# A mixture-of-experts step on one core: the order of the weight loads of each turn, the slot of the last fixed expert, and the place of the sort that orders the experts

## The chip, the cores and the metric

The kernel runs as one program on one core of a Trainium2 chip. The metric is the device time in microseconds of one execution, the median of three runs of the kernel before. Everything is 32-bit floating point.

## The reference

One step of a two-layer backbone over 128 context tokens and 128 latent tokens, 1024 wide. Each layer mixes tokens (retention, differential attention, latent attention), then runs a mixture of experts. Only the second half matters here:

```python
scores = jax.nn.sigmoid(x @ router_w)              # (256 tokens, 64 experts)
sel = scores + router_bias                          # best 4 of 8 groups, then top 6 experts
gates = scores[eidx] / sum * ROUTED_SCALE
for e in experts:                                   # 64 experts, hidden width 256
    y += gate_e * (silu(x_e @ w_gate[e]) * (x_e @ w_up[e])) @ w_down[e]
y += swiglu(x, sh_w_gate, sh_w_up, sh_w_down)       # shared expert
x = x + gate2 * y
```

Each expert has three matrices of 1 MiB (gate, up, down). All 64 experts of both layers are read: 384 MiB. Which tokens go to which expert is known only at run time.

## The kernel before

Below, a *block* is one of those 1 MiB matrices, moved by one DMA. All blocks are issued by SyncE (SP), whose DMA queue serves them.

**Rounds.** A layer's experts are done in 22 rounds. Experts 0 to 3 are fixed and fill rounds 0 and 1, two experts each. Then come ten turns of two rounds: a *quad round* (four experts, at most 32 tokens each) and a *pair round* (two experts, at most 64 tokens each). The 60 experts of the turns are sorted by token count at run time, and the sorted list `order_i` names the expert that a load takes.

**Slots.** There are five places for an expert's three blocks. A quad round uses slots 0, 1, 2, 3. A pair round uses slot 4 (the fifth: `fifth_gate`, `fifth_up`, `fifth_dn`) and slot 0. So slot 0 is loaded twice in a turn: for the quad, and for the pair's second expert. Slots 1, 2, 3 and 4 are loaded once. That is 18 blocks a turn. In what follows Q0 to Q3 are the quad's experts, P4 and P0 the pair's, and a part is named behind them, as in "P0 up".

**TensorE in a round** (`expert_round`, L1808 to L1861; the matmuls of gate and up are L1832, those of down L1861). Gate matmuls, up matmuls, the first half of the next round's token gather (L1764), the scatter of the round before (L1771), transposes (L1399), the second half of the gather, and then the down matmuls. Two rounds of a layer have something *between* the scatter and the transposes: the pair round of turn 1 runs the shared expert's up matmuls (L1729), and the pair round of turn 2 its down matmuls (L1808). TensorE tells SyncE three things in each round: gate done, up done, down done (`used[0]`, `used[1]`, `used[2]`).

**SyncE in a turn** (the loop at L629). A slot's part may be loaded once the round that used it has said that it is done with it. SyncE is in order: what stands behind a wait is not issued before it. The expert's number comes into a register by `expert_in` (L469), a read of `order_i` in on-chip memory. The loop's body first reads seven of them.

**The start of a layer's experts.** The first three fixed experts are loaded before the router runs. The last one waits for the normalised activations: its gate goes into `fifth_gate`, its down into `fifth_dn`, its up into the first half of a `gu` slot, which the shared expert's gate weights occupy until `sh_gate` (L596 to L600). Meanwhile VectorE ranks the experts (L1284 to L1286, semaphore `ranked`), TensorE multiplies the ranking out (L1756, `ordered`) and VectorE writes `order_i` (L1293, `order_ready`).

Of the kernel before, what the change touches and what calls it, by code (L numbers as in the profile page):

```python
# [31 lines left out]
NC_ = D // P  # L32
G = 2
# [13 lines left out]
E = 64  # L47
GROUPS = 8
TOP_G, TOP_K = 4, 6
FF = 256  # L50
# [4 lines left out]
FIXED = 4  # L55
TURNS = 10
QUAD_CAP, PAIR_CAP = 32, 64
ROUNDS = 2 + 2 * TURNS
PER_TURN = 6
# [7 lines left out]
def quad_at(m):  # L67
    return FIXED + PER_TURN * m


def pair_at(m):
    return FIXED + PER_TURN * m + 4
# [4 lines left out]
CO = {n: P * i for i, n in enumerate(CONSTS)}  # L77
COL = {"i+1": 0, "C-i": 1, "C-1-i": 2, "i": 3, "eps": 4, "sel": 5, "first": 13, "cap": 16}
# [86 lines left out]
def trunk(nc, t, out):  # L165
    ctx = ExitStack()
    with ctx:
# [7 lines left out]
        RING = 4  # L175
        gu = sb("gu", [P, RING, 2 * NC_ * FF])
        dn = sb("dn", [P, RING, 2, D])
        cst = sb("cst", [P, FIRST_W])
# [110 lines left out]
        key_row, above, chosen = (hit[0:E, E * n:E * n + E] for n in range(3))  # L289
# [13 lines left out]
        fifth_gate = xh[:, 0].rearrange("p c t -> p (c t)")  # L303
        fifth_up, fourth_up = carve(NC_ * FF), carve(NC_ * FF)
        fifth_dn = carve(2 * D).rearrange("p (j n) -> p j n", j=2)
        fourth_dn = carve(2 * D).rearrange("p (j n) -> p j n", j=2)

        PS = ctx.enter_context(nc.psum_tensor("PS", [P, 8, 512], F32))
# [56 lines left out]
        S = {n: sem(n) for n in names}  # L365
# [12 lines left out]
        item_slot, expert_slot = {}, []  # L378
# [88 lines left out]
        def expert_in(sp, l, at):  # L467

            return sp.value_load(order_i[0:1, l, at], min_val=0, max_val=E - 1)  # L469
# [28 lines left out]
        def _(sp):  # L498
            def gate_or_up(l, x, half):
                return t[f"exp_w_{('gate', 'up')[half]}"][l, bass.ds(x, 1)].rearrange("e (p c) n -> (e p) (c n)", c=NC_)  # L500
# [20 lines left out]
            def load_fixed_dn(j, l):  # L521
                sp.dma_start(dn_block(j if j < RING - 1 else RING), down(l, j)).then_inc(S["fixed_dn_in"], 16)

            def load_quad(j, l, x, part):
                if part == 2:
                    sp.dma_start(dn_block(j), down(l, x)).then_inc(S["quad_dn_in"], 16)
                else:
                    sp.dma_start(gu_block(j, l, part), gate_or_up(l, x, part)
                                 ).then_inc(S["quad_up_in" if part else "quad_gate_in"], 16)

            def load_pair(j, l, x, part):
                if part == 2:
                    sp.dma_start(dn_block(j), down(l, x)).then_inc(S["pair_dn_in"], 16)
                else:
                    sp.dma_start(gu_block(j, l, part), gate_or_up(l, x, part)
                                 ).then_inc(S["pair_up_in" if part else "pair_gate_in"], 16)
# [3 lines left out]
            for l in range(DEPTH):  # L540

                for n in range(starts[l], ends[l]):
# [8 lines left out]
                    slot = item_slot[n]  # L551
# [39 lines left out]
                    if j == 2:  # L591
                        load_fixed_dn(2, l)

                last, slot = FIXED - 1, expert_slot[l][RING - 1]
                sp.wait_ge(S["h_a"], NC_ * (2 * l + 2))
                sp.wait_ge(S["h_d"], NC_ * (2 * l + 2))  # L596
                sp.dma_start(fifth_gate, gate_or_up(l, last, 0)).then_inc(S["last_fixed_in"], 16)
                load_fixed_dn(last, l)
                sp.wait_ge(S["sh_gate"], l + 1)
                sp.dma_start(gu[:, slot, 0:NC_ * FF], gate_or_up(l, last, 1)).then_inc(S["last_fixed_in"], 16)  # L600


                r0, used = ROUNDS * l, [S[n] for n in ("gate_done", "up_done", "down_done")]
                sp.wait_ge(S["order_ready"], l + 1)
                xs = [expert_in(sp, l, slice(quad_at(0) + j, quad_at(0) + j + 1)) for j in range(4)]
                xf = expert_in(sp, l, slice(pair_at(0), pair_at(0) + 1))
                xp = expert_in(sp, l, slice(pair_at(0) + 1, pair_at(0) + 2))

                load_quad(3, l, xs[3], 1)
                load_pair(RING, l, xf, 1)  # L610
                load_quad(3, l, xs[3], 2)

                for part in range(3):
                    sp.wait_ge(used[part], r0 + 1)
# [4 lines left out]
                load_pair(RING, l, xf, 0)  # L619
                sp.wait_ge(used[1], r0 + 2)  # L620
                load_quad(2, l, xs[2], 1)
                load_quad(3, l, xs[3], 0)
                sp.wait_ge(used[2], r0 + 2)
                load_quad(2, l, xs[2], 2)
                load_pair(RING, l, xf, 2)
                for part in range(2):
                    sp.wait_ge(used[part], r0 + 3)
                    load_pair(0, l, xp, part)
                with sp.Fori(0, TURNS - 1) as m:  # L629
                    xs = [expert_in(sp, l, bass.ds(m * PER_TURN + (quad_at(1) + j), 1)) for j in range(4)]  # L630
                    xl = expert_in(sp, l, bass.ds(m * PER_TURN + (pair_at(0) + 1), 1))
                    xf = expert_in(sp, l, bass.ds(m * PER_TURN + pair_at(1), 1))
                    xp = expert_in(sp, l, bass.ds(m * PER_TURN + (pair_at(1) + 1), 1))

                    for part in range(2):
                        sp.wait_ge(used[part], m * 2 + (r0 + 3))
                        for j in range(1, 4):
                            load_quad(j, l, xs[j], part)
                    sp.wait_ge(used[2], m * 2 + (r0 + 3))
                    load_pair(0, l, xl, 2)  # L640

                    for part in range(2):
                        sp.wait_ge(used[part], m * 2 + (r0 + 4))
                        load_quad(0, l, xs[0], part)
                    for j in range(1, 4):
                        load_quad(j, l, xs[j], 2)
                    sp.wait_ge(used[2], m * 2 + (r0 + 4))
                    load_quad(0, l, xs[0], 2)
                    for part in range(2):
                        load_pair(RING, l, xf, part)  # L650

                        sp.wait_ge(used[part], m * 2 + (r0 + 5))
                        load_pair(0, l, xp, part)
                    load_pair(RING, l, xf, 2)
                xl = expert_in(sp, l, slice(pair_at(TURNS - 1) + 1, pair_at(TURNS - 1) + 2))
                sp.wait_ge(used[2], r0 + ROUNDS - 1)
                load_pair(0, l, xl, 2)
                over_loads(sp, l)


# [273 lines left out]
        def _(v):  # L934
# [81 lines left out]
            for l in range(DEPTH):  # L1016
# [208 lines left out]
                for g in range(G):  # L1225
                    for a in range(GROUPS):
                        last = v.max(gtop[:, g, a], selv[:, g, 8 * a:8 * a + 8])
# [33 lines left out]
                r0, g0, s0_ = ROUNDS * l, ROUNDS * l, ROUNDS * l  # L1261
# [10 lines left out]
                def one_hot(b, n, at, fixed=False):  # L1272

                    return tt(onehot[b].rearrange("p g (e s) -> p g e s", e=n), iota_of(n),
                              fixed_columns(posu, n, at) if fixed else columns(pos, n, at), ALU.is_equal)
# [4 lines left out]
                              fixed_columns(score, n, at) if fixed else columns(wgt, n, at), ALU.mult)  # L1280

                v.tensor_copy(counts, PS[0:E, 6, 0:2])
                one_hot(0, 2, 0, True).then_inc(S["sel_ready"], 1)
                link(ts(above, key_row, key_col, None, ALU.is_gt))  # L1284
                link(v.tensor_reduce(rank, above, AX.X, ALU.add))
                ts(chosen, cst[0:E, order + E:order + 2 * E], rank, None, ALU.is_equal).then_inc(S["ranked"], 1)  # L1286
                settle("ranked")
                v.wait_ge(S["sel_ready"], s0_ + 1)
                gate_it(0, 2, 0, True).then_inc(S["gated_ready"], 1)
                one_hot(1, 2, 2, True).then_inc(S["sel_ready"], 1)  # L1290
# [104 lines left out]
        def _(pe):  # L1395
# [66 lines left out]
            for l in range(DEPTH):  # L1462
# [264 lines left out]
                def shared_part(bank, u, j, ks):  # L1727
                    for k in ks:
                        ins = mmul(PS[:, bank, j * T:j * T + T], w[:, u, k, j], hT[:, k, :], start=(k == 0),  # L1729
                                   stop=(k == NC_ - 1))  # L1730
                    return ins
# [11 lines left out]
                ins.then_inc(S["tallied"], 1)  # L1743

                shared_part(5, 0, 1, range(4))
                pe.wait_ge(S["weighed"], l + 1)
                pe.wait_ge(S["placed"], l + 1)
                for a, x in enumerate((posu, score)):
                    for g in range(G):
                        ins = turn(PS[0:E, 7, (2 * a + g) * P:(2 * a + g + 1) * P], x[:, g])  # L1750
                ins.then_inc(S["counted"], 1)
                shared_part(5, 0, 1, range(4, NC_)).then_inc(S["sh_gate"], 1)

                pe.wait_ge(S["ranked"], l + 1)
                pe.wait_ge(S["h_tok_a"], G * (l + 1))
                mmul(PS[0:2, 2, 0:E], cst[0:E, CO["cols"] + COL["i"]:CO["cols"] + COL["i"] + 2], chosen,  # L1756
                     start=True, stop=True).then_inc(S["ordered"], 1)

                r0, g0 = ROUNDS * l, ROUNDS * l

# [51 lines left out]
                def block_of(x):  # L1812
                    return x.rearrange("p (k n) -> p k n", k=NC_)
# [6 lines left out]
                def expert_round(m, u, gus, dns, gates_in, ups_in, downs_in, last=False, between=None):  # L1820
# [37 lines left out]
                    for n in range(2):  # L1858
                        for j in range(2):
                            for h, weights in enumerate(dns):  # L1860
# [5 lines left out]
                own = [gate_up(j) for j in range(RING)]  # L1866
                fixed_in = [(gu_loaded[expert_slot[l][j]], fixed_at[l][j]) for j in range(RING - 1)]
                expert_round(0, 0, own[0:2], (dn[:, 0], dn[:, 1]), fixed_in[0:2], [], (S["fixed_dn_in"], 64 * l + 64))
                expert_round(0, 1, (own[2], (block_of(fifth_gate), own[3][0])), (dn[:, 2], fifth_dn),
                             [fixed_in[2], (S["last_fixed_in"], 32 * l + 32)], [], (S["fixed_dn_in"], 64 * l + 64))  # L1870
                t0 = TURNS * l + 1
                quad_gus = own[0:3] + [(own[3][0], block_of(fourth_up))]
# [120 lines left out]
```

## Time and profile before

| what | value |
|---|---|
| median of three runs | 1432.39 us (1431.57 to 1439.19) |
| the profiled execution, its own time | 1434.13 us |
| its span in the trace | 1432.3 us |
| TensorE matmul busy | 1289.1 us (90%) |
| VectorE, ScalarE busy | 287.6 us, 239.4 us |
| bytes moved | 496.18 MB, mean 346 GB/s |
| mean granted TensorE clock | 0.939 of full |
| chain that ended last | PE 69%, DMA 23% |

A busy TensorE is not one at its peak, and an engine that waits for data still shows a high share when the clock is low while it works. A DMA is shown twice: when its queue issues it, and, in the view of the DMA issues, how long it took from there until its data had landed. The profiled execution is 1.7 us above the median.

### The profile page before, as it was taken

The page shows a single profiled execution, that of the slowest core. Times are in us where ns is not written, and L with a number is a line of the kernel's source. Part 1 is how long each engine was busy: PE and PEld are TensorE (multiplying, and loading weights), DVE is VectorE, ACT ScalarE, POOL GpSimd, SP SyncE. Part 2 cuts the span into 40 slices and gives each one's busy share as a digit, 9 for nine tenths or more (in the row PEclk, how much of TensorE's full clock was granted, in tenths as well). Part 3 has the DMA queues.
Part 4 walks back from the last instruction along what each step waited for, and adds up shares of the span by engine and source line. Part 5 has one row for each costly group of instructions (what it writes and reads, how often), then busy time and mean ns, then how long its engine had stood idle before and what let it go on. Part 6 is the DMA issues. An engine that isn't in the chain of part 4 may idle for free.

```text
span 1432.3 us, 23390 instructions
## 1 busy us (share of the span) xinstructions
PE 1289.1 (90%) x9852; PEld 886.9 (62%) x9852; DVE 287.6 (20%) x694; ACT 239.4 (17%) x500; POOL 2.6 (0%) x13
## 2 busy tenths in 40 slices
PE   5999989999997998889999988999999888889886
PEld 2665678766674655556566557876676645556554
DVE  1306414111101101011041442321101101011012
ACT  1112513111000110010130253211100000001001
POOL 0000000000000000000000000000000000000000
PEclk8999779999998999999899997999999989999998
DMA  9866636989999999999973671398999999999992
GB/s 392 318 248 257 258 147 265 381 355 420 421 420 422 422 422 422 422 422 422 392 262 136 244 312 60 164 387 337 422 421 421 421 422 421 422 421 422 423 421 94
DMA packets 81026, 496.18 MB, mean 346 GB/s; under 512 B 10560, under 2 KB 12864, under 8 KB 24640
## 3 DMA queue, kind: packets, MB, share of 16 engines
q1 hardware_dynamic: 76752, 492.68, 84.2%
q10 hardware_dynamic: 4208, 2.52, 0.6%
q8 instruction: 53, 0.87, 0.2%
q14 instruction: 13, 0.11, 0.0%
HBM read 493.17 MB, written 2.00 MB: 346 GB/s over the span
## 4 chain that ended last, share of the span: by engine, by line
PE 69%; DMA 23%; DVE 3%; ACT 3%; issue 1%; SPq 0%; DVEq 0%; ACTq 0%
DMA dn<-in_exp_w_down 20%; PE PS L1832 15%; PE PS L1861 12%; PE PS L1458 9%; PE PS L1764 7%; PE PS L1771 7%; PE PS L1701 4%; PE PS L1399 3%; PE PS L1729 2%; DMA gu<-in_w_ada 2%; DMA gu<-in_exp_w_gate 2%; ACT xh L839 2%; PE PS L1431 2%; PE PS L1684 1%; PE PS L1808 1%
## 5 line engine op out<-in xcount | busy, mean ns | idle before, releaser
L1832 PE MATMUL PS<-gu,arena 128*32 128x256 f32 (+1 forms) x3104 | 313.4, 380 | 4.6 <-DMA gu<-in_exp_w_gate 2.8
L1861 PE MATMUL PS<-arena 128*64 128x512 f32 (+1 forms) x336 | 178.8, 682 | 84.0 <-DMA dn<-in_exp_w_down 77.9
L1832 PEld LDWEIGHTS PS<-gu,arena 128*32 128x32 f32 (+1 forms) x3104 | 186.3, 117 | 79.9 <-issue 23.0
L1861 PE MATMUL PS<-dn,arena 128*32 128x512 f32 (+1 forms) x688 | 186.7, 638 | 0.0
L1764 PE MATMUL PS<-arena 128*128 128x128 f32 x1408 | 176.5, 278 | 0.5 <-ACT arena L892 0.5
L1764 PEld LDWEIGHTS PS<-arena 128*128 128x128 f32 x1408 | 163.9, 192 | 18.0 <-issue 16.7
L1771 PE MATMUL PS<-arena 128*128 128x256 f32 x704 | 159.6, 380 | 1.4 <-ACT arena L874 1.4
L1832 PE MATMUL PS<-arena 128*32 128x256 f32 (+1 forms) x640 | 144.8, 379 | 1.5 <-DMA gu<-in_exp_w_up 1.5
L1771 PEld LDWEIGHTS PS<-arena 128*128 128x128 f32 x704 | 130.4, 190 | 19.8 <-ACT arena L874 3.2
L874 ACT ACTIVATE arena<-PS 128x512 f32<-128x512 f32 x88 | 52.5, 597 | 486.7 <-PE PS L1861 486.7
L1317 DVE TENSOR_TENSOR arena<-arena,PS 128x256 f32<-128x256 f32 x44 | 18.5, 421 | 564.3 <-ACT arena L888 564.3
L1861 PEld LDWEIGHTS PS<-arena 128*64 128x64 f32 (+1 forms) x336 | 44.6, 144 | 138.3 <-issue 136.3
L1832 PEld LDWEIGHTS PS<-arena 128*32 128x32 f32 (+1 forms) x640 | 78.9, 123 | 25.2 <-DMA gu<-in_exp_w_up 2.4
L1832 PE MATMUL PS<-xh,arena 128*64 128x256 f32 x352 | 80.6, 382 | 0.0
L1861 PEld LDWEIGHTS PS<-dn,arena 128*32 128x32 f32 (+1 forms) x688 | 48.4, 127 | 45.7 <-issue 42.8
L1311 DVE COPY arena<-PS 128x512 f32<-128x512 f32 x44 | 30.4, 691 | 214.5 <-PE PS L1399 214.5
L1832 PEld LDWEIGHTS PS<-xh,arena 128*64 128x64 f32 x352 | 46.6, 137 | 37.0 <-issue 15.1
L888 ACT ACTIVATE arena<-PS 128x256 f32<-128x256 f32 x44 | 16.9, 383 | 297.1 <-PE PS L1832 297.1
L1458 PE MATMUL PS<-gu,xh 128*128 128x512 f32 (+1 forms) x192 | 65.0, 497 | 0.0
L1458 PE MATMUL PS<-xh,gu 128*128 128x256 f32 x256 | 59.0, 393 | 1.2 <-DVE xh L974 1.2
L1701 PE MATMUL PS<-xh,gu 128*128 128x256 f32 x256 | 58.6, 393 | 0.0
L1458 PEld LDWEIGHTS PS<-xh,gu 128*128 128x128 f32 x256 | 50.4, 198 | 10.7 <-issue 3.4
(225 smaller groups left out, 1051.7 us busy)
## 6 DMA issues: line engine op xcount, KB each, us to landing
gu<-in_exp_w_gate SPq DMA_DIRECT2D x106, 1024.0 KB, 12.6
gu<-in_exp_w_up SPq DMA_DIRECT2D x88, 1024.0 KB, 15.6
dn<-in_exp_w_down SPq DMA_DIRECT2D x86, 1024.0 KB, 19.5
gu<-in_w_ada SPq DMA_DIRECT2D x24, 2048.0 KB, 10.5
arena<-in_exp_w_down SPq DMA_DIRECT2D x42, 1024.0 KB, 16.1
arena<-in_exp_w_up SPq DMA_DIRECT2D x40, 1024.0 KB, 14.7
xh<-in_exp_w_gate SPq DMA_DIRECT2D x22, 1024.0 KB, 10.6
gu<-in_w_in SPq DMA_DIRECT2D x8, 2048.0 KB, 15.3
```

Source lines behind the costliest of these rows:

```text
L839: A(prob[:, m, 0:nk * P], PS[:, m // 2, (m % 2) * 256:(m % 2) * 256 + nk * P], ACT.Exp, bias=small[:, 340 + m:341 + m], scale=scale, accum ...
L874: return A(yy[:, :, half], PS[:, 7 - n, :].rearrange("p (t c) -> p c t", c=NC_), ACT.Copy)
L1311: return v.tensor_copy(turned_back, PS[:, 6, :])
L1399: return pe.transpose(dst, src, ident[0:parts, 0:parts])
L1431: ins = mmul(PS[32 * j:32 * j + 32, 7, :], condw[:, 2 * quarter + c, :], wv[:, c, 512 * j:512 * j + 512], start=(quarter == 0 and c == 0), ...
L1458: ins = mmul(PS[0:lhs(k).shape[-1], bank, o:o + rhs(k).shape[-1]], lhs(k), rhs(k), start=(k == 0), stop=(k == NC_ - 1))
L1701: ins = mmul(PS[:, wo_bank(c), (c % 2) * T:(c % 2) * T + T], wo[k // 4][:, k % 4, c], mixT[:, k], start=(k == 0), stop=(k == NC_ - 1))
L1729: ins = mmul(PS[:, bank, j * T:j * T + T], w[:, u, k, j], hT[:, k, :], start=(k == 0), stop=(k == NC_ - 1))
L1764: ins = mmul(PS[:, 4, (c % 4) * P:(c % 4) * P + P], h_tok[:, g, c], onehot[b][:, g], start=(g == 0), stop=(g == 1))
L1771: ins = mmul(PS[:, c // 2, (c % 2) * T:(c % 2) * T + T], yy[:, c], selT, start=(first and c % 2 == 0), stop=False, skip_group_check=True)
L1832: ins = mmul(PS[w * h:w * h + w, 5, FF * half:FF * half + FF], xg[:, k, w * h:w * h + w], weights[half][:, k], start=(k == 0), stop=(k == ...
L1861: ins = mmul(PS[w * h:w * h + w, 7 - n, :], hidT[:, j * P + w * h:j * P + w * h + w], weights[:, j, 512 * n:512 * n + 512], start=(j == 0) ...
```

## The change

The diff does four things.

1. The last fixed expert lies wholly in slot 4: its up goes to `fifth_up`, with no wait for `sh_gate`. Round 1 reads it there.
2. Before the turns, SyncE reads one register, loads all of Q3 (up, down, then gate behind the wait for `sh_gate`), and reads four more. P4 up is loaded later, behind the up of round 1.
3. In a turn, the loads of P0 gate and up are moved. Before, they stood at the end of the body that belongs to the turn before. Now they stand at the head of their own turn's body, and the loads of Q1 to Q3 for the next turn follow each of them. P4 gate, up and down are issued together. The body reads six registers, ahead of its waits. P0's down stays where it is. The last turn's P0 loads stand behind the loop.
4. On VectorE the ranking goes ahead of the first one-hot matrix. On TensorE the product with the ranking goes ahead of the transposes that `placed` and `weighed` release.

```diff
-                last, slot = FIXED - 1, expert_slot[l][RING - 1]
                 sp.wait_ge(S["h_a"], NC_ * (2 * l + 2))
                 sp.wait_ge(S["h_d"], NC_ * (2 * l + 2))
-                sp.dma_start(fifth_gate, gate_or_up(l, last, 0)).then_inc(S["last_fixed_in"], 16)
-                load_fixed_dn(last, l)
-                sp.wait_ge(S["sh_gate"], l + 1)
-                sp.dma_start(gu[:, slot, 0:NC_ * FF], gate_or_up(l, last, 1)).then_inc(S["last_fixed_in"], 16)
+                for half in range(2):
+                    sp.dma_start(gu_block(RING, l, half), gate_or_up(l, FIXED - 1, half)).then_inc(S["last_fixed_in"], 16)
+                load_fixed_dn(FIXED - 1, l)
...
-                xs = [expert_in(sp, l, slice(quad_at(0) + j, quad_at(0) + j + 1)) for j in range(4)]
+                x3 = expert_in(sp, l, slice(quad_at(0) + 3, quad_at(0) + 4))
+                load_quad(3, l, x3, 1)
+                load_quad(3, l, x3, 2)
+                sp.wait_ge(S["sh_gate"], l + 1)
+                load_quad(3, l, x3, 0)
                 xf = expert_in(sp, l, slice(pair_at(0), pair_at(0) + 1))
-                xp = expert_in(sp, l, slice(pair_at(0) + 1, pair_at(0) + 2))
-
-                load_quad(3, l, xs[3], 1)
-                load_pair(RING, l, xf, 1)
-                load_quad(3, l, xs[3], 2)
+                xs = [expert_in(sp, l, slice(quad_at(0) + j, quad_at(0) + j + 1)) for j in range(3)] + [x3]
...
                 load_quad(2, l, xs[2], 1)
-                load_quad(3, l, xs[3], 0)
+                load_pair(RING, l, xf, 1)
...
-                for part in range(2):
-                    sp.wait_ge(used[part], r0 + 3)
-                    load_pair(0, l, xp, part)
                 with sp.Fori(0, TURNS - 1) as m:
...
                     for part in range(2):
                         sp.wait_ge(used[part], m * 2 + (r0 + 3))
+                        load_pair(0, l, xl, part)
                         for j in range(1, 4):
                             load_quad(j, l, xs[j], part)
...
                     load_quad(0, l, xs[0], 2)
-                    for part in range(2):
+                    for part in range(3):
                         load_pair(RING, l, xf, part)
-
-                        sp.wait_ge(used[part], m * 2 + (r0 + 5))
-                        load_pair(0, l, xp, part)
-                    load_pair(RING, l, xf, 2)
                 xl = expert_in(sp, l, slice(pair_at(TURNS - 1) + 1, pair_at(TURNS - 1) + 2))
-                sp.wait_ge(used[2], r0 + ROUNDS - 1)
-                load_pair(0, l, xl, 2)
+                for part in range(3):
+                    sp.wait_ge(used[part], r0 + ROUNDS - 1)
+                    load_pair(0, l, xl, part)
...
-                one_hot(0, 2, 0, True).then_inc(S["sel_ready"], 1)
                 link(ts(above, key_row, key_col, None, ALU.is_gt))
                 link(v.tensor_reduce(rank, above, AX.X, ALU.add))
                 ts(chosen, cst[0:E, order + E:order + 2 * E], rank, None, ALU.is_equal).then_inc(S["ranked"], 1)
                 settle("ranked")
+                one_hot(0, 2, 0, True).then_inc(S["sel_ready"], 1)
```

The queue of SyncE, layer 0, from the head of the loop's body to the first block of the next quad. Line 535 loads gate or up of a pair's expert, 528 those of a quad's, 526 and 533 their downs; the name before the arrow is the place. Before:

```order
L469 TENSOR_LOAD order_i
L469 ISA x2
L636 ISA
L528 ISA
L528 DMA gu<-in_exp_w_gate 128x2048
L528 ISA
L528 DMA gu<-in_exp_w_gate 128x2048
L528 ISA
L528 DMA gu<-in_exp_w_gate 128x2048
L528 DMA gu<-in_exp_w_up 128x2048 x2
L528 DMA arena<-in_exp_w_up 128x2048
L533 DMA dn<-in_exp_w_down 128x2048
```

After:

```order
L469 TENSOR_LOAD order_i
L469 ISA x2
L632 ISA
L535 ISA
L535 DMA gu<-in_exp_w_gate 128x2048
L528 ISA
L528 DMA gu<-in_exp_w_gate 128x2048
L528 ISA
L528 DMA gu<-in_exp_w_gate 128x2048
L528 ISA
L528 DMA gu<-in_exp_w_gate 128x2048
L535 DMA gu<-in_exp_w_up 128x2048
```

P0 gate now stands ahead of the three quad gates, and P0 up behind them. The end of the body, SyncE again, before:

```order
L526 DMA dn<-in_exp_w_down 128x2048
L535 ISA
L535 DMA xh<-in_exp_w_gate 128x2048
L652 REGISTER_ALU
L535 ISA
L535 DMA gu<-in_exp_w_gate 128x2048
L535 DMA arena<-in_exp_w_up 128x2048
L535 DMA gu<-in_exp_w_up 128x2048
L533 DMA arena<-in_exp_w_down 128x2048
```

After:

```order
L526 DMA dn<-in_exp_w_down 128x2048
L535 ISA
L535 DMA xh<-in_exp_w_gate 128x2048
L535 DMA arena<-in_exp_w_up 128x2048
L533 DMA arena<-in_exp_w_down 128x2048
```

P0 gate and up (the two into `gu`) have left this place; the three blocks of P4 stand together behind Q0's down.

## Rows read from the trace of the kernel before

**Rows 1.** The page of the execution: moved GB/s in 40 equal slices.

```profile
GB/s 392 318 248 257 258 147 265 381 355 420 421 420 422 422 422 422 422 422 422 392 262 136 244 312 60 164 387 337 422 421 421 421 422 421 422 421 422 423 421 94
```

**Rows 2.** Windows of a loaded stretch: us busy of each engine (x), granted clock, DMA share, GB/s.

```profile
400.00:480.00 80.00, 69.43 (x606) 48.69 (x605) 8.65 (x18) 7.12 (x13) 0.00 (x0) 0.94 1.01 421
```

**Rows 3.** Waits of TensorE, 290 to 700 us: total, times, longest.

```profile
PE PS L1861 <- DMA dn<-in_exp_w_down: 40.9, 7, 8.6
...
PE PS L1832 <- DMA gu<-in_exp_w_gate: 0.8, 1, 0.8
```

**Rows 4.** Timeline of the DMA queue, layer 0, one turn: start, duration, issue.

```profile
510.39 0.33 SPq L526 DMA_DIRECT2D dn<-in_exp_w_down  x1
...
514.14 0.33 SPq L535 DMA_DIRECT2D gu<-in_exp_w_gate  x1
...
523.31 1.37 SPq L528 DMA_DIRECT2D gu<-in_exp_w_gate  x3
...
528.84 0.33 SPq L533 DMA_DIRECT2D dn<-in_exp_w_down  x1
532.43 0.33 SPq L528 DMA_DIRECT2D gu<-in_exp_w_gate  x1
535.74 0.33 SPq L528 DMA_DIRECT2D gu<-in_exp_w_up  x1
...
554.96 0.33 SPq L526 DMA_DIRECT2D dn<-in_exp_w_down  x1
```

**Rows 5.** Timeline of TensorE in the same turn.

```profile
535.63 2.05 PE L1764 MATMUL PS<-arena 128*128 128x128 f32 x16
...
541.42 1.95 PE L1764 MATMUL PS<-arena 128*128 128x128 f32 x16
549.57 1.08 PE L1861 MATMUL PS<-arena 128*64 128x512 f32 x1 [6.19 <-DMA dn<-in_exp_w_down]
```

**Rows 6.** DMA issues at 528.8 us: KB, us from issue to landing.

```profile
dn<-in_exp_w_down SPq DMA_DIRECT2D x1, 1024.0 KB, 20.6
```

**Rows 7.** DMA issues at 254.3 us, into an empty queue.

```profile
arena<-in_exp_w_up SPq DMA_DIRECT2D x1, 1024.0 KB, 4.7
```

**Rows 8.** Timeline of the DMA queue, layer 0, first turn.

```profile
290.08 0.33 SPq L526 DMA_DIRECT2D dn<-in_exp_w_down  x1
...
294.67 0.33 SPq L535 DMA_DIRECT2D gu<-in_exp_w_gate  x1
297.99 0.33 SPq L535 DMA_DIRECT2D gu<-in_exp_w_up  x1
303.18 1.37 SPq L528 DMA_DIRECT2D gu<-in_exp_w_gate  x3
```

**Rows 9.** Windows at the two layers' first turns.

```profile
290.00:292.00 2.00, 1.22 (x26) 0.91 (x28) 0.00 (x0) 0.60 (x1) 0.00 (x0) 1.00 0.43 82
290.00:310.00 20.00, 19.22 (x222) 13.62 (x222) 2.47 (x5) 2.77 (x5) 0.00 (x0) 1.00 0.84 320
...
980.00:1000.00 20.00, 18.47 (x214) 13.18 (x216) 2.47 (x5) 1.81 (x5) 0.00 (x0) 1.00 0.80 301
```

**Rows 10.** Timeline of the DMA queue, layer 1, first turn.

```profile
979.58 0.33 SPq L526 DMA_DIRECT2D dn<-in_exp_w_down  x1
...
985.38 0.33 SPq L535 DMA_DIRECT2D gu<-in_exp_w_gate  x1
...
994.23 1.65 SPq L528 DMA_DIRECT2D gu<-in_exp_w_gate  x3
```

**Rows 11.** Timeline of TensorE, layer 0, turn 1, in its pair round.

```profile
358.64 7.07 PE L1729 MATMUL PS<-xh,gu 128*128 128x256 f32 x32
```

**Rows 12.** Windows at the starts of three down steps of pair rounds.

```profile
504.00:506.00 2.00, 1.20 (x4) 0.59 (x6) 0.00 (x0) 0.00 (x0) 0.00 (x0) 0.50 0.99 414
549.00:551.00 2.00, 1.44 (x4) 0.59 (x6) 0.00 (x0) 0.00 (x0) 0.00 (x0) 0.50 1.04 434
413.00:415.00 2.00, 1.20 (x6) 0.57 (x8) 0.33 (x1) 0.00 (x0) 0.00 (x0) 1.00 1.02 426
```

More of the change, by code:

```diff
@@ L625, in _ @@
                 load_pair(RING, l, xf, 2)
-                for part in range(2):
-                    sp.wait_ge(used[part], r0 + 3)
-                    load_pair(0, l, xp, part)
                 with sp.Fori(0, TURNS - 1) as m:
+                    xl = expert_in(sp, l, bass.ds(m * PER_TURN + (pair_at(0) + 1), 1))
                     xs = [expert_in(sp, l, bass.ds(m * PER_TURN + (quad_at(1) + j), 1)) for j in range(4)]
-                    xl = expert_in(sp, l, bass.ds(m * PER_TURN + (pair_at(0) + 1), 1))
                     xf = expert_in(sp, l, bass.ds(m * PER_TURN + pair_at(1), 1))
-                    xp = expert_in(sp, l, bass.ds(m * PER_TURN + (pair_at(1) + 1), 1))
                     for part in range(2):
                         sp.wait_ge(used[part], m * 2 + (r0 + 3))
+                        load_pair(0, l, xl, part)
                         for j in range(1, 4):
@@ L1745, in _ @@
                 shared_part(5, 0, 1, range(4))
+                pe.wait_ge(S["ranked"], l + 1)
+                pe.wait_ge(S["h_tok_a"], G * (l + 1))
+                mmul(PS[0:2, 2, 0:E], cst[0:E, CO["cols"] + COL["i"]:CO["cols"] + COL["i"] + 2], chosen, start=True,
+                     stop=True).then_inc(S["ordered"], 1)
                 pe.wait_ge(S["weighed"], l + 1)
@@ L1752, in _ @@
                 shared_part(5, 0, 1, range(4, NC_)).then_inc(S["sh_gate"], 1)
[L1754 to L1757, printed above, removed]
                 r0, g0 = ROUNDS * l, ROUNDS * l
@@ L1868, in _ @@
                 expert_round(0, 0, own[0:2], (dn[:, 0], dn[:, 1]), fixed_in[0:2], [], (S["fixed_dn_in"], 64 * l + 64))
-                expert_round(0, 1, (own[2], (block_of(fifth_gate), own[3][0])), (dn[:, 2], fifth_dn),
+                expert_round(0, 1, (own[2], (block_of(fifth_gate), block_of(fifth_up))), (dn[:, 2], fifth_dn),
                              [fixed_in[2], (S["last_fixed_in"], 32 * l + 32)], [], (S["fixed_dn_in"], 64 * l + 64))
```

## The prediction

> **What bounds the kernel now.** I read the page's row of moved bytes first [rows 1]. It has two long plateaus at 420 to 423 GB/s, one in each layer's turns, and nothing higher anywhere. A window inside one says the same: 421 GB/s with the DMA engines busy all the time, while TensorE shows 69.4 of 80 us [rows 2]. The waits of TensorE name the data: 40.9 us in 7 waits on down blocks, up to 8.6 us each, and almost nothing on gates [rows 3]. Then one turn in the queue's timeline [rows 4]: the down of Q0 is issued at 510.39 and 554.96, so a turn takes 44.57 us for 18 blocks, 2.476 us a block. TensorE needs less. From the issue at 510.39 (pair's down done) the quad round takes 18.45 us to 528.84, the pair's gates 3.6 to 532.43, its ups 3.3 to 535.74. Gather, scatter and transposes take 7.6 more, to 543.4 [rows 5], and a down step at full clock about 3.7. That is 36.7 us; the rest of the turn is idle time, and it stands at the pair's down, which waits 6.19 us for the P0 block until 549.57 [rows 5]. P0's down was issued at 528.84 and took 20.6 us to land [rows 6], against 4.7 us for a block in an empty queue [rows 7]: some eight blocks were ahead. So the blocks are served in turn, and a layer ends when its stream of blocks ends. Only two things can move the time: an empty queue in the stream, and the TensorE work behind the last blocks.
>
> **The start of the turns: a gain.** In layer 0 the queue is empty around 290 (82 GB/s from 290 to 292) [rows 9], so whatever was issued before has landed, in whichever order. Parts 1, 2 and 4 of the change therefore only shift work inside an interval that ends in an empty queue. Counted block by block, the 16 that both kernels issue between the first three fixed experts and 290 are the same set, apart from the last fixed up in another place. I cost them at nothing. The cover is TensorE's own path through rounds 0 and 1, which sets 290.08 [rows 8]. If it is gone they are worth at most one wait for a gate, 0.8 us [rows 3], either way.
>
> From 290.08 on, the kernel before issues in trickles: two blocks, one at 294.67, one at 297.99, then seven register reads (5 us) before the gates of the next quad at 303.18 [rows 8]. From 290 to 310 it moves 320 GB/s [rows 9], a shortfall of (421-320)/421 x 20 = 4.8 us. Of that 1.6 us is the lead-in after the empty queue, which stays ((421-82)/421 x 2) [rows 9]. Changed, the six reads end near 290.9 + 6 x 0.7 = 295.1, and four blocks follow at once, while two are still moving to 297. I leave 0.3 us of gap: gain 4.8 - 1.6 - 0.3 = 2.9 us. In layer 1 the same places are 979.58, 985.38 and 994.23 [rows 10] and the rate is 301 GB/s [rows 9]: shortfall 5.7 us, gain 5.7 - 1.6 - 0.3 = 3.8 us. Bounds of both together: 4 us, if part of the lag belongs to single slow DMA engines that an empty queue lets catch up, to 7.5 us.
>
> In the steady turns the seventh read and the earlier issues are worth nothing. At 554.96, where the queue is shortest, the blocks issued behind P0's down still have 5 x 2.476 - 5.4 = 7 us to go; that is the cover.
>
> **The place of P0 up: a loss.** Changed, the order of service is P4's three, P0 gate, Q1 to Q3 gate, P0 up, Q1 to Q3 up, P0 down, Q0 gate, Q0 up, Q1 to Q3 down, Q0 down. P0 up had Q1 to Q3's gates behind it and now has them ahead. It lands four blocks before P0 down, 9.9 us, instead of eight. Call P0 up's landing zero. TensorE then needs ups 3.3, the middle 7.6 and downs 3.7, 14.6 us, until it releases Q0's down. The stream behind P0 up holds 9 blocks, 22.3 us, and a block issued into an empty queue starts 4.7 - 2.5 = 2.2 us late. So SyncE must issue by 20.1. In a plain turn 5.5 us are to spare and nothing is lost.
>
> Two pair rounds of each layer have 6.9 us of shared-expert matmuls in the middle (7.07 us in the row) [rows 11]. There the chain is 21.5 us, 1.4 us past the limit, and the stream stands still for 1.4 us. Before the change these rounds waited only for P0's down, which has 5 blocks behind it (limit 10.2 us) and 3.7 to 5.4 us of work: no loss.
>
> The clock adds to it. Where TensorE had idled for 6 us the granted clock is 0.50 (1.2 GHz) at 504 and 549; at 413, after the round with the shared downs, where it had hardly idled, it is 1.00 (2.4 GHz) [rows 12]. Between 549.57 [rows 5] and 554.96 [rows 4] the downs took 5.4 us instead of 3.7: 1.7 us dearer. Changed, turn 1 waits about 5.5 us, now ahead of the ups (gates done at 290.1 + 36.7 + 22.0 = 348.8; P0 up landing 23 blocks behind P4's down of turn 0, which lands at 290.1 + 4.7 + 2.5 = 297.3, so 354.2). I take 1.7 us there (bounds 0 and 3.4), and nothing in turn 2, whose wait falls to 2.5 us because turn 1 ran late.
>
> At the end of a layer the last P0 gate, up and down are late for nobody, as before. But the pair round of turn 8 now ends 14.6 + 1.7 - 9.9 = 6.4 us behind P0 down's landing instead of 5.4: +1.0 us (bounds -1.7, if the clock stays up, and +2).
>
> **Sum.** Layer 0: -2.9 + 1.4 + 1.7 + 1.4 + 1.0 = +2.6. Layer 1: -3.8 + 1.4 + 1.7 + 1.4 + 1.0 = +1.7. Together +4.3 us. On the profiled execution, 1434.13 us, that gives 1438.4; the median of the runs is 1.7 lower, so 1436.7 us.
>
> **A rule about order.** The row shows 20.6 us for a block with eight ahead [rows 6], which speaks for service in turn. The Trainium skill says in "DMA: Bandwidth & Descriptors", section "Queues, rings and completion order", that each DMA engine takes descriptors in the order of its ring, but that completion is not first in, first out for an issuing engine, because later ones may finish before earlier ones. By its second half P0 up could land with the gates ahead of it, which is the first rival below. By its first half the sum stands, and the trace agrees with that half.
>
> **Rivals.**
> *P0 up is not late enough to matter*, since blocks overlap in service or the clock stays up. For it: near the starts single blocks take longer than a block's time, so engines do not run in step. Against it: the 20.6 us. Then only the start gain counts, less up to 1 us: 1432.4 - 6.7 = 1425.7 us.
> *Every turn runs the queue dry* (slower). The slow stretch lasts through ups and scatter, 3 us or more, so downs are done at 17.6; together with two or three slow DMA engines the 20.1 us limit is passed, and 2 us more go in each between-round. It decides from a chain of 20.1 us. Place: the issue of Q0's down, 8 turns a layer. With 3 us twice a layer and 1 us at the tail beyond my terms: (2 x (1.3 + 1.3) + 1 + 1) on top of +4.3, some +11: 1444 us.
> *The change reaches nothing*: the start gain is eaten by the lag of the slowest DMA engine, and the shared matmuls stay covered by the same lag. 1432 us.
>
> **Chances.** Forecast 0.60 (own range 1432 to 1441), first rival 0.16, second 0.14, third 0.10. About 0.5%, 7.2 us, is what a measurement of this kernel can tell from no change. Below 1425.2 lies half of the first rival: 0.08. Above 1439.6 lie the second rival and a little of the forecast: 0.16. The rest is 0.76. The range takes in the forecast and most of both sides: 1426 to 1443.
>
> **What would show it.** Right: between 292 and 303 the changed kernel moves about 421 GB/s, and TensorE's waits for data stand at the up matmuls, not at the downs. Right: the queue is empty for 1 to 4 us after the pair rounds of turns 1 and 2 in each layer, and the half clock falls on the ups. Wrong: P0 up lands less than 3 us behind P0 gate; no gap at turns 1 and 2 (the time is then 1426 to 1430); gaps in later turns (then 1442 and more); or a start of round 0 that moved by over 1 us, which I cost at nothing.

## The result and the profile after

The changed kernel is slower: 1447.69 us median (1444.03 to 1452.71, 6 runs) against 1434.97 us before (1431.57 to 1439.19, 6 runs). The ratio is 1.0091, 95% interval 1.0068 to 1.0114. I had forecast 1436.7 us with a range up to 1443; the direction was right, the loss is 12.7 us instead of 4.3. (The forecast started from 1432.39 us, the median of the first three of these six runs of before.) The profiled execution took 1444.03 us, with a span of 1442.2, so 9.9 us above the span of before. Single executions of one kernel differ by some microseconds in stretches that nothing changed (the first expert load of layer 1 follows the last of layer 0 by other amounts). So I read the turns by themselves: from the release of Q2's down of the first turn to the release of Q0's down of the last. In layer 0 that was 290.08 to 690.34 before and is 287.43 to 693.49 now, in layer 1 979.58 to 1380.68 and 983.73 to 1390.25: 5.8 and 5.4 us longer, 11.2 together.

The page of the changed kernel, moved GB/s in 40 slices; this answers to [rows 1]:

```profile
GB/s 392 332 252 257 269 107 320 352 415 421 373 358 423 421 421 422 422 422 422 398 245 128 271 283 59 189 397 384 420 350 422 369 421 422 422 422 422 422 421 95
```

Each plateau now has two dents at its start, 373 and 358, 350 and 369, where it had 420 and more before. They are turns 1 and 2 of each layer. The waits of TensorE over the whole execution:

```profile
PE PS L1825 <- DMA gu<-in_exp_w_up: 86.5, 16, 6.3
```

In [rows 3] the waits were at the down matmuls; now they are at the up matmuls (L1825), and the downs wait for no data at all. The timeline of the DMA queue, layer 0, turns 1 and 2 (start us, duration, issue; L526 are downs of quads, the single one that of Q0, L533 downs of pairs):

```profile
358.48 0.33 SPq L528 DMA_DIRECT2D gu<-in_exp_w_up  x1
358.90 0.86 SPq L526 DMA_DIRECT2D dn<-in_exp_w_down  x2
359.85 0.38 SPq L526 DMA_DIRECT2D arena<-in_exp_w_down  x1
376.64 0.33 SPq L526 DMA_DIRECT2D dn<-in_exp_w_down  x1
...
394.94 0.33 SPq L533 DMA_DIRECT2D dn<-in_exp_w_down  x1
398.66 0.33 SPq L528 DMA_DIRECT2D gu<-in_exp_w_gate  x1
408.75 0.33 SPq L528 DMA_DIRECT2D gu<-in_exp_w_up  x1
409.18 0.86 SPq L526 DMA_DIRECT2D dn<-in_exp_w_down  x2
410.13 0.39 SPq L526 DMA_DIRECT2D arena<-in_exp_w_down  x1
426.91 0.33 SPq L526 DMA_DIRECT2D dn<-in_exp_w_down  x1
```

The issue at 359.85 and the one at 410.13 are the last blocks in the queue before Q0's down. The view of the DMA issues at the first of these two, at Q0's down, and at the two blocks issued behind it, at 377.15 and 377.58 (KB, us to landing):

```profile
arena<-in_exp_w_down SPq DMA_DIRECT2D x1, 1024.0 KB, 15.8
...
dn<-in_exp_w_down SPq DMA_DIRECT2D x1, 1024.0 KB, 4.7
...
xh<-in_exp_w_gate SPq DMA_DIRECT2D x1, 1024.0 KB, 6.7
arena<-in_exp_w_up SPq DMA_DIRECT2D x1, 1024.0 KB, 10.1
```

The first landed at 375.7, Q0's down was issued at 376.64, after that. It landed in the 4.7 us of an empty queue [rows 7], at 381.3, where it would have landed at 378.1 in an unbroken stream: the stream stood still for 3.2 us. In turn 2 the same two landings are 425.0 and 431.6: 4.1 us. In layer 1 the same reading gives 4.8 us in turn 1 and 3.3 in turn 2. These four are the only blocks of the changed kernel's turns that SyncE issued after everything ahead of them had landed. Windows of the changed kernel (us, busy of each engine, granted clock, DMA share, GB/s):

```profile
287.40:307.40 20.00, 20.00 (x230) 13.27 (x232) 2.47 (x5) 2.77 (x5) 0.00 (x0) 1.00 0.95 389
350.00:352.00 2.00, 0.00 (x0) 0.00 (x0) 0.00 (x0) 0.00 (x0) 0.00 (x0) 0.50 1.00 418
...
376.00:380.00 4.00, 4.00 (x68) 2.11 (x68) 0.00 (x0) 0.60 (x1) 0.00 (x0) 1.00 0.57 195
400.00:402.00 2.00, 0.00 (x0) 0.00 (x0) 0.00 (x0) 0.00 (x0) 0.00 (x0) 0.65 1.01 410
402.00:404.00 2.00, 1.25 (x6) 0.77 (x8) 0.00 (x0) 0.00 (x0) 0.00 (x0) 0.50 0.98 410
404.00:406.00 2.00, 2.00 (x12) 1.15 (x10) 0.00 (x0) 0.00 (x0) 0.00 (x0) 0.50 1.03 430
```

The first row is the gain: 389 GB/s in the 20 us in which the kernel before moved 320 [rows 9]. The third is the standstill: 195 GB/s. The second and fourth show TensorE idle and the granted clock going down to 0.50 (1.2 GHz) ahead of the ups, in turn 1 and also in turn 2; in the last two the ups run at 0.50. TensorE's timeline at turn 2:

```profile
402.75 0.69 PE L1825 MATMUL PS<-arena 128*64 128x256 f32 x1 [4.26 <-DMA gu<-in_exp_w_up]
```

It waited 4.26 us there and then took 6.0 us for its ups (402.7 to 408.75) instead of the 3.3 of the forecast.

### The profile page after: what moved, and what is told of

Read it like the earlier page. It is cut to its first block, busy times and chain, and to the rows that moved or that the text cites. A ratio compares the mean times of both kernels' runs of the same rounds, so it can differ in the third digit from the quotient of the medians.

```text
span 1442.2 us, 23272 instructions
## 1 busy us (share of the span) xinstructions
PE 1294.1 (90%) x9852; PEld 889.7 (62%) x9852; DVE 287.7 (20%) x694; ACT 239.7 (17%) x500; POOL 2.7 (0%) x13
## 4 chain that ended last, share of the span: by engine, by line
PE 59%; DMA 24%; SPq 7%; DVE 4%; issue 3%; ACT 3%; DVEq 0%; ACTq 0%
DMA gu<-in_exp_w_up 21%; PE PS L1825 12%; PE PS L1452 8%; PE PS L1757 7%; PE PS L1854 7%; PE PS L1764 6%; PE PS L1695 4%; SPq L469 3%; PE PS L1393 3%; PE PS L1723 2%; ACT xh L833 2%; DMA gu<-in_w_ada 2%; SPq L535 1%; SPq L528 1%; PE PS L1425 1%
## 5 line engine op out<-in xcount | busy, mean ns | idle before, releaser
L1825 PE MATMUL PS<-gu,arena 128*32 128x256 f32 (+1 forms) x3072 | 349.6, 393 | 1.8 <-issue 1.8
L1825 PE MATMUL PS<-arena 128*64 128x256 f32 (+1 forms) x672 | 185.9, 439 | 86.5 <-DMA gu<-in_exp_w_up 86.5
L1825 PEld LDWEIGHTS PS<-gu,arena 128*32 128x32 f32 (+1 forms) x3072 | 198.3, 122 | 77.9 <-issue 19.5
L1825 PEld LDWEIGHTS PS<-arena 128*64 128x64 f32 (+1 forms) x672 | 97.1, 147 | 132.6 <-DMA gu<-in_exp_w_up 93.8
L1757 PEld LDWEIGHTS PS<-arena 128*128 128x128 f32 x1408 | 164.1, 192 | 17.9 <-issue 16.7
L1854 PE MATMUL PS<-dn,arena 128*32 128x512 f32 (+1 forms) x688 | 160.2, 596 | 0.0
L1854 PE MATMUL PS<-arena 128*64 128x512 f32 (+1 forms) x336 | 152.6, 597 | 1.6 <-DVE arena L1305 1.6
L1825 PE MATMUL PS<-xh,arena 128*64 128x256 f32 x352 | 80.5, 382 | 3.1 <-DMA gu<-in_exp_w_gate 3.1
L1825 PEld LDWEIGHTS PS<-xh,arena 128*64 128x64 f32 x352 | 46.6, 137 | 39.0 <-issue 13.3
L1854 PEld LDWEIGHTS PS<-dn,arena 128*32 128x32 f32 (+1 forms) x688 | 42.2, 118 | 45.6 <-issue 42.8
L1854 PEld LDWEIGHTS PS<-arena 128*64 128x64 f32 (+1 forms) x336 | 38.2, 123 | 38.5 <-issue 34.3
## 6 DMA issues: line engine op xcount, KB each, us to landing
gu<-in_w_ada SPq DMA_DIRECT2D x24, 2048.0 KB, 10.8
```

Of the source, the lines that this page charges most:

```text
L1757: ins = mmul(PS[:, 4, (c % 4) * P:(c % 4) * P + P], h_tok[:, g, c], onehot[b][:, g], start=(g == 0), stop=(g == 1))
L1825: ins = mmul(PS[w * h:w * h + w, 5, FF * half:FF * half + FF], xg[:, k, w * h:w * h + w], weights[half][:, k], start=(k == 0), stop=(k == ...
L1854: ins = mmul(PS[w * h:w * h + w, 7 - n, :], hidT[:, j * P + w * h:j * P + w * h + w], weights[:, j, 512 * n:512 * n + 512], start=(j == 0) ...
```

## The experiments

All ratios, and all distances from before, are against runs of the kernel before on the same chip. A distance from the changed kernel is the difference of two such distances, since it was not run beside them; it is rounded. How long "the turns" were is read as above, in the profiled execution. "Place" is my theory: P0 up, behind the gates of Q1 to Q3, starts a chain (ups, middle, downs) that is longer than the stream behind it where the shared expert's matmuls stand in the middle.

**start_only.** The turns' loads as before, with the changed start.

```diff
+                for part in range(2):
+                    sp.wait_ge(used[part], r0 + 3)
+                    load_pair(0, l, xp, part)
                 with sp.Fori(0, TURNS - 1) as m:
...
-                        load_pair(0, l, xl, part)
```

> The start of the changed kernel (last fixed expert in slot 4, Q3 loaded whole, ranking first) with the turns' loads as before. Theory 'place' (P0 up behind the quad's gates makes the chain to Q0's down too long in the rounds with shared matmuls): 0 us against before, within 1.5. Theory 'start' (the moved start costs): most of the 12.7 us, +8 or more.

Measured 1430.99 us, ratio 0.9985 (0.9968 to 1.0001). The start costs nothing, so theory "start" falls. If anything it gains, 3.2 us by the medians, more than the 1.5 I allowed: in the trace the turns were 4.3 us shorter than before, and TensorE had no wait for a gate in the first quad rounds. The kernel before has one there in each layer, 0.8 us in layer 0 [rows 3] and 2.0 in layer 1:

```profile
PE PS L1832 <- DMA gu<-in_exp_w_gate: 2.8, 2, 2.0
```

The median's gain is not clear of no change.

**turns_only.** The start as before, with the changed turns.

```diff
-                for part in range(2):
-                    sp.wait_ge(used[part], r0 + 3)
-                    load_pair(0, l, xp, part)
...
+                        load_pair(0, l, xl, part)
                         for j in range(1, 4):
                             load_quad(j, l, xs[j], part)
```

> The start as before, the turns' loads of the changed kernel. Theory 'place': all of the loss, +10 to +14 us against before, with an empty queue after the pair rounds of turns 1 and 2. Theory 'start': +4 or less.

Measured 1450.39 us, ratio 1.0109 (1.0083 to 1.0135), 16 us above before, 2 more than I had expected at most. All of the loss is here. With the 3 us that start_only gained, the two halves add up to the whole, 13 us. Two blocks in each layer, behind the pair rounds of turns 1 and 2, were issued into an empty queue, as in the changed kernel; start_only has none.

**up_ahead.** One order of the changed kernel undone.

```diff
                     for part in range(2):
                         sp.wait_ge(used[part], m * 2 + (r0 + 3))
                         load_pair(0, l, xl, part)
+                    for part in range(2):
                         for j in range(1, 4):
                             load_quad(j, l, xs[j], part)
```

> The changed kernel with one order undone: P0 gate and P0 up are both issued ahead of the gates of Q1 to Q3, whose gates and ups follow. Reads in front and P4's three blocks together stay. Theory 'place': the loss goes and the gain at the start stays: 5 to 8 us below before. A rival 'P4' (P4's three blocks together, ahead of P0 gate, are what makes the pair round late): still 8 or more above before.

Measured 1429.61 us, ratio 0.9976 (0.9956 to 0.9997): 4.6 us below before by the medians, 17 below the changed kernel. No block was issued into an empty queue. Rival "P4" falls. The gain is just under the 5 to 8 us that I expected; in its trace the turns were 3.1 and 3.5 us shorter than before, as forecast, but its runs scatter from 1422.65 to 1439.22. Its waits are at the downs again:

```profile
PE PS L1855 <- DMA dn<-in_exp_w_down: 60.6, 12, 5.2
PE PS L1826 <- DMA gu<-in_exp_w_gate: 17.8, 14, 2.5
```

**shared_in_quad.** The changed kernel with the shared matmuls in the quad rounds of turns 1 and 2. VectorE's part of the shared expert moves with them (its lines are left out below).

```diff
...
-                    quad(m)
-                    pair(m, between=shared_up if m == UP_TURN else shared_down if m == DOWN_TURN else None)
+                    quad(m, between=shared_up if m == UP_TURN else shared_down if m == DOWN_TURN else None)
+                    pair(m)
```

> The changed kernel with the shared expert's up and down matmuls done in the quad rounds of turns 1 and 2, not in their pair rounds. Theory 'place': the chain behind P0 up is 6.9 us shorter in turns 1 and 2, the queue is never empty there, 12 to 16 us less than the changed kernel, so 0 to 4 below before. Theory 'start' or 'P4': as slow as the changed kernel, +10 or more.

Measured 1427.41 us (1424.76 to 1429.20), ratio 0.9952 (0.9933 to 0.9971), 6.8 us below before, more than I expected, and 20 below the changed kernel. P0 up is as late as in the changed kernel, and TensorE waits for ups all the same, 74.1 us in all:

```profile
PE PS L1825 <- DMA gu<-in_exp_w_up: 74.1, 16, 6.3
```

But the chain behind it no longer has the 6.9 us. In its queue's timeline Q0's down of turn 2 is issued at 366.41, 10.8 us behind the downs before it (355.58), where the changed kernel took 17.7, and no block was issued into an empty queue:

```profile
355.58 0.86 SPq L526 DMA_DIRECT2D dn<-in_exp_w_down  x2
...
366.41 0.33 SPq L526 DMA_DIRECT2D dn<-in_exp_w_down  x1
```

This kernel beats both the kernel before and the changed one.

**up_behind.** The kernel before with P0 up alone behind the quad's gates.

```diff
-                    for part in range(2):
-                        load_pair(RING, l, xf, part)
-
-                        sp.wait_ge(used[part], m * 2 + (r0 + 5))
-                        load_pair(0, l, xp, part)
+                    load_pair(RING, l, xf, 0)
+                    sp.wait_ge(used[0], m * 2 + (r0 + 5))
+                    load_pair(0, l, xp, 0)
+                    load_pair(RING, l, xf, 1)
...
+                        if part == 1:
+                            load_pair(0, l, xl, 1)
                         for j in range(1, 4):
```

> The kernel before with P0 up alone moved: it is issued behind the gates of Q1 to Q3 of the next turn, everything else as before. Theory 'place': this one block carries the whole loss, and the start of the turns stays as it was, so +12 to +18 us against before. Rival 'P4': P4's blocks standing together share in it: +6 or less.

Measured 1456.01 us, ratio 1.0156 (1.0139 to 1.0174): 22 us above before. One block's place carries the whole loss. I had expected up to 18. Its four standstills add up to 16.1 us, about the changed kernel's 15.4; that it comes out above turns_only fits the start of the turns, where it gains little (P0's down of turn 0 lands 34.3 and 34.5 us behind the release of Q2's down, in turns_only 31.2 and 32.4). Its turns were 17.9 us longer than before; the other 4 us I can't explain. Its longest wait for an up is 8.1 us, where the changed kernel's is 6.3:

```profile
PE PS L1833 <- DMA gu<-in_exp_w_up: 94.0, 18, 8.1
```

**filler, filler_again and its control filler_tiny.** The changed kernel with spare matmuls while TensorE waits for P0 up in turns 1 and 2; in the control they are 2 columns wide.

```diff
...
                         ins.then_inc(S["up_done" if half else "gate_done"], 1)
+                        for _ in range(0 if half else filler):
+                            mmul(PS[:, 5, FF:2 * FF], ident, cst[:, 0:FF], start=True, stop=True)
...
+                         filler={UP_TURN: 11, DOWN_TURN: 8}.get(m, 0))
```

> The changed kernel with 11 and 8 spare matmuls (results not used) between gates and ups of the pair rounds of turns 1 and 2, where TensorE waits for P0 up; the output stays the same. Theory 'clock' (the half clock on the ups, 2 to 3 us in each of these rounds, is most of what my forecast lacked): ups take 3.3 to 3.7 us there, the empty stretches shrink, 6 to 10 us below the changed kernel. Rival 'order alone' (the chain is too long at any clock): no more than 2 us below it.

The first time 1447.57 us, ratio 1.0097 (1.0077 to 1.0117): some 1 us above the changed kernel, against my expectation. In the trace, though, the clock stayed up, the ups took 3.7 us after their wait, and the turns were 2.9 and 4.0 us shorter than in the changed kernel. The time had gone elsewhere: ahead of the last pair round of each layer, which in the program stands behind a branch, TensorE stood for 2.2 and 2.6 us without a releaser and began at half clock. So I ran it again beside a control of the same program length.

> The kernel of the run 'filler' once more, beside its control. In its trace the turns were 7 us shorter than in the changed kernel, but TensorE stood 2.2 and 2.6 us for no shown reason ahead of the last pair round of each layer and began it at half clock. Both theories: about 1447 us, as the first time.

> The control: the same 19 spare matmuls a layer, at the same places, each of 2 columns instead of 256, so that the program is as long but TensorE still idles. Theory 'clock and code place' (the full clock saves 7 us, and the longer program costs as much ahead of the last pair round): 6 to 8 us above filler_again. Rival 'the clock is worth nothing': as filler_again, within 2 us.

Measured 1448.81 us, ratio 1.0113 (1.0085 to 1.0142), and 1455.66 us, ratio 1.0147 (1.0112 to 1.0182). The control is 6.9 us slower, in the expected 6 to 8. Windows of filler_again in turn 2 of layer 0:

```profile
400.00:402.00 2.00, 2.00 (x11) 1.74 (x10) 0.00 (x0) 0.00 (x0) 0.00 (x0) 1.00 1.06 442
402.00:404.00 2.00, 1.46 (x10) 0.86 (x10) 0.00 (x0) 0.00 (x0) 0.00 (x0) 1.00 0.95 393
404.00:406.00 2.00, 2.00 (x22) 1.30 (x19) 0.00 (x0) 0.00 (x0) 0.00 (x0) 1.00 1.08 451
```

Clock 1.00 where the changed kernel had 0.50 to 0.65, so the half clock on the ups of the four pair rounds with shared matmuls is worth about 7 us. The intervals of the two ratios overlap, so the size rests on the medians and on the traces: from filler_tiny to filler_again the turns are 4.7 and 3.8 us shorter, and each of the four standstills is 1.8 us, where filler_tiny has 3.2 to 4.8. The clock is not all of it: with the clock up the turns are still 3.5 us longer than before, although they start with the changed kernel's gain. So the order costs time at full clock too. The stall ahead of the last pair round of layer 1 of filler_again, the only wait of TensorE from 1400 to 1412 us:

```profile
PE PS L1825 <- issue: 2.5, 1, 2.5
```

**both.** up_ahead and shared_in_quad together.

```diff
+                    for part in range(2):
                         for j in range(1, 4):
                             load_quad(j, l, xs[j], part)
...
-                    quad(m)
+                    quad(m, between=shared_up if m == UP_TURN else shared_down if m == DOWN_TURN else None)
```

> P0 gate and up ahead of the quad gates, and the shared matmuls in the quad rounds. If the two repairs remove the same loss, nothing is left to add: 5 to 8 us below before, as the better of the two alone. If moving the shared matmuls also helps where P0 up is early, 9 or more below.

Measured 1429.84 us (1423.20 to 1438.78), ratio 0.9967 (0.9952 to 0.9981), 3.9 below. Nothing is added: the two repairs remove the same loss. That the gain is smaller than 5 to 8, and scatters like up_ahead's, I can't explain; in the profiled execution, its slowest, the turns were 7.6 us shorter than before, but they began 5.9 us later, and 5.5 us more passed between the layers' turns.

**before_in_quad.** The kernel before with the same move of the shared matmuls, VectorE's part included.

```diff
...
-                    quad(m)
-                    pair(m, between=shared_up if m == UP_TURN else shared_down if m == DOWN_TURN else None)
+                    quad(m, between=shared_up if m == UP_TURN else shared_down if m == DOWN_TURN else None)
+                    pair(m)
```

> The kernel before with the shared matmuls in the quad rounds. Theory 'place': nothing was lost in these rounds before, so within 1.5 us of before. Rival 'shared matmuls cost in the pair rounds in any order': 4 us or more below.

Measured 1434.02 us, ratio 1.0006 (0.9992 to 1.0021). No change. The shared matmuls cost in the pair rounds only where P0 up is late.

**spare_before and spare_after.** Sixteen spare matmuls in the middle of the pair rounds of turns 3 to 8, where neither kernel loses anything otherwise.

```diff
+                def spare():
+                    for _ in range(16):
+                        mmul(PS[:, 7, 0:FF], ident, cst[:, 0:FF], start=True, stop=True)
                 with pe.Fori(DOWN_TURN + 1, TURNS - 1) as m:
                     quad(m)
-                    pair(m)
+                    pair(m, between=spare)
```

> The kernel before with 16 spare matmuls (6.9 us, results not used) in the middle of the pair rounds of turns 3 to 8. P0's down is the last thing waited for and has 5 blocks behind it: theory 'place' says the 6.9 us fit in the idle time, so 0 to 4 us above before. Rival 'TensorE bounds these turns as well': 12 x 3 us or more.

> The same spare matmuls in the changed kernel. Theory 'place': each of these 12 pair rounds now has the long chain, so each runs the queue dry and loses what turn 2 lost (standstill and restart, 4 to 6 us): 45 to 75 us above the changed kernel. Rival (turns 1 and 2 lose for another reason, such as the shared weights): under 15 us above it.

Measured 1441.36 us, ratio 1.0056 (1.0021 to 1.0090), and 1503.75 us, ratio 1.0492 (1.0461 to 1.0523). The same work costs 8.9 us in the old order. In the new one it costs 59 us (71 us above before, less the changed kernel's 13), 4.9 us in each of the 12 rounds, and the trace has 16 blocks issued into an empty queue, one behind each pair round of turns 1 to 8 in both layers. One window of each, spare_before first:

```profile
500.00:600.00 100.00, 96.47 (x847) 67.90 (x849) 11.93 (x24) 9.89 (x18) 0.00 (x0) 1.00 1.01 422
```

```profile
500.00:600.00 100.00, 91.59 (x762) 63.55 (x760) 9.89 (x20) 8.71 (x16) 0.00 (x0) 0.96 0.95 393
```

The stream stays at 422 GB/s in the one and falls to 393 in the other. The 8.9 us of spare_before, more than the 4 I allowed, are not in its turns (287.51 to 686.66 and 983.79 to 1382.13, 1.1 and 2.8 us shorter than before). They are at the last pair rounds again, 3.6 us of stall ahead of that of layer 0 and 4.3 ahead of that of layer 1, with the rounds slowed behind them. From 1395 to 1410 us:

```profile
PE PS L1832 <- issue: 4.3, 1, 4.3
```

## Why the prediction was wrong

The mechanism was right, and its sizes were not. By the steps:

- *The start of the turns.* Forecast -2.9 and -3.8 us. P0's down of turn 0 lands 31.0 us behind the release of Q2's down, before it was 34.2; in layer 1 31.2 and 35.8. So -3.2 and -4.6. The turns' loads alone (turns_only) give -6.4 of these -7.8: right.
- *Parts 1, 2 and 4 at nothing.* On top of the turns' loads they give the other -1.4 us. By themselves (start_only) they give -3.1 at this place. My bound of 0.8 us came from rows of layer 0 alone; layer 1's wait for a gate was 2.0. Nearly right.
- *The chain.* Forecast 1.4 us past the limit in each of the four rounds. With the clock up (filler_again) each standstill was 1.8: after a wait the ups take 3.7 us, not 3.3. Nearly right, 0.4 short each time.
- *The clock in turn 1.* I took 1.7 us (bounds 0 and 3.4). The ups took 5.1 us in layer 0 and 6.6 in layer 1, 1.4 and 2.9 more than 3.7. The standstills were 3.2 and 4.8 us, forecast 3.1.
- *Turn 2: the step that failed.* I wrote "nothing in turn 2, whose wait falls to 2.5 us", and priced its round at 1.4. It waited 4.26 us, the clock had fallen to half all the same, the ups took 2.3 us more than 3.7, and the standstill was 4.1 us (3.3 in layer 1). I let the clock fall only after a wait of about 6 us, since the two rows that I had were one of 6.2 and one of hardly any; the rest lay between, and I took the better end. Even a wait near 2.5 us was no ground for nothing: in spare_after the waits for P0 up in turns 4 to 8 were 2.8 to 3.0 us (layer 0, turn 4 below), and the ups behind them took 5.1 to 6.7.
- *The restart of the queue, a term that I put at nothing.* Behind an empty queue a block lands late once. The block issued at 377.15 landed 6.7 us later, at 383.8, and the one at 377.58 took 10.1 us, to 387.7: 3.8 us behind the first instead of 2.5. I had seen this at the layer starts and used it only as a bound of the gain. Here it came behind each of the four standstills, 1.3 to 1.4 us each, 5.4 together. In turn 1 it also brought P0 up of turn 2 later (402.7), which lengthened that wait.
- *The tail.* Forecast +1.0 in each layer; measured +0.3 and +0.7 between P0's down and the release of Q0's down in the last turns.

```profile
503.59 0.45 PE L1825 MATMUL PS<-arena 128*64 128x256 f32 x1 [2.78 <-DMA gu<-in_exp_w_up]
```

Standstills 15.4 us, gain -7.8, tail 1.0: 8.6 of the 11.2 us that the turns are longer. Of the other 2.6, 2.4 are in the landings: the four restarts of 5.4 us in all, less 3.0 us by which the stream of the kernel before slips without an empty queue, once in each layer behind the pair round of turn 2 (the block issued at 417.49 lands 1.5 us late, at 430.1). Why it slips there is open. These 11.2 us lie within the interval of the ratio, 9.8 to 16.4 us.

The range failed for the same reason. Its upper end, 1443, came from the second rival, "every turn runs the queue dry", to which I gave 0.14. Plain turns did not run dry, so this rival is false as stated. That the price came out near it is luck, since turn 2 of each layer lost two to three times what I had given it. A bound for the clock of 3.4 us in one turn a layer was too narrow: it belonged on both.

## What to carry to other kernels

Where a stream of loads bounds a loop, look at each block for the chain that it starts: from its landing through the work that releases the next buffer, against the blocks that are still queued behind it. The rounds with extra work decide, not the plain ones; here 6.9 us of other work in two pair rounds of ten made an order of loads lose 3 to 5 us in each, and moving that work to a round with slack turned a loss of 12.7 us into a gain of 6.8 against before. When a wait moves, price what runs after it at half clock, unless the trace shows waits of that length with the clock still up, and count the late block behind every empty queue.

## What the runs showed of the hardware

A wait of 4.26 us was enough for the granted clock to fall to 0.65 and then 0.50 in the windows above, and to keep the following matmuls at 0.50 for over 3 us. Shorter waits went both ways: the clock fell after those of 2.8 to 3.0 us in spare_after, and stayed at 1.00 around one of 3.1 us in shared_in_quad (ahead of the gates at 1120.9).

A longer program for TensorE cost time at one place far from the added instructions. Ahead of the last pair round of each layer, behind the branch, it stood 2.2 to 3.2 us in the three filler kernels, 3.6 and 4.3 us in spare_before, and 1.1 and 1.9 us in spare_after. In the fillers and spare_before the clock was low after it, and the gates and ups of that round took 8.5 to 10.1 us instead of 7.1. No releaser is shown there, and neither kernel without the additions has it. The traces have a hint of the cause: in each of the eight stalls of the fillers and spare_before, one packet of 16 KB on the queue for instructions (q8) starts between 0.5 us before the stall and 1.6 us into it, and TensorE goes on 1.4 to 1.8 us after it ends. For spare_before, layer 1, from 1401.9 to 1403.2 us:

```profile
q8 instruction: 1, 0.02, 5.3%
```

In the kernel before, the last such packet of layer 0 ahead of that round starts at 701.4, 7.2 us before the round. That TensorE waited for these instructions is likely, but no run tests it.

A median can hide a gain behind such a stall. Without the control, filler would have read as "the clock is worth nothing".
